# Five input projections a layer from one-pass products of two parts, and a last expert unit by column halves

## The reference, cut to what matters

```
(a_q, a_k, a_v, a_g, a_lr, b_u, c_q, c_k, c_v, c_qi, c_ki, c_wi, d_uv) = split_cols(z, IN_SPLITS)
o_a = gla_mixer(a_q, a_k, a_v, a_g, a_lr, ...)
o_b = pool_mixer(b_u, ...)
o_c = dsa_mixer(c_q, c_k, c_v, c_qi, c_ki, c_wi, rel_bias)   # top 64 keys a query, then attention
o_d = sgu_mixer(d_uv, ...)
h += concatenate([o_a, o_b, o_c, o_d]) @ W_out
```

## Time and profile before

| what | value |
|---|---|
| median of 3 runs | 1337.87 us (1337.4 to 1337.96) |
| the profiled execution | 1337.72 us, of which the span is 1335.9 us |
| PE busy | 1256.2 us (94% of the span) |
| DVE, ACT, POOL busy | 500.4, 379.0, 85.1 us |
| input projections and mixers, layer 0 and layer 1 | about 11 to 137 us, 366 to 486 us |
| dense feed-forward of layer 0 | about 175 to 360 us |
| experts | about 537 us to the end |
| idle time of PE in front of expert matmuls, ended by a DMA | 35.2 and 26.5 us |

### The profile page before, as it was taken

The page is one execution under the profiler, slowest core; times in us unless marked ns, Lnnn a source line. Parts: engine busy times, 40 slices in busy tenths (PEclk is TensorE's granted clock), DMA queues, the critical chain, the costliest instruction groups (busy, mean ns, idle before and its releaser), DMA issues.

```text
span 1335.9 us, 15465 instructions
## 1 busy us (share of the span) xinstructions
PE 1256.2 (94%) x6128; PEld 758.1 (57%) x6128; DVE 500.4 (37%) x886; ACT 379.0 (28%) x603; POOL 85.1 (6%) x69
## 2 busy tenths in 40 slices
PE   8999999999999999999989789889889999999876
PEld 6868888888887787434324224224226888434222
DVE  2736387777653726301001001001006999101002
ACT  2542454444424413101001001001005887101002
POOL 0570000000007300000000000000000000000000
PEclk9999999999999999999999999889889999999999
DMA  9733515442473179799999999999999999899996
GB/s 342 315 126 111 220 54 231 174 163 90 146 294 116 43 276 369 326 428 435 426 434 429 432 429 435 428 432 432 432 432 425 429 427 426 370 428 426 429 429 263
DMA packets 32650, 435.81 MB, mean 326 GB/s; under 512 B 5260, under 2 KB 7376, under 8 KB 9296
## 3 DMA queue, kind: packets, MB, share of 16 engines
q1 hardware_dynamic: 32400, 434.48, 78.4%
q0 software_dynamic: 192, 0.53, 0.1%
HBM read 433.94 MB, written 1.05 MB: 326 GB/s over the span
## 4 chain that ended last, share of the span: by engine, by line
PE 68%; DMA 27%; DVE 2%; ACT 1%; SPq 1%; issue 1%; DVEq 0%
DMA ring<-in_experts 26%; PE bank L2256 14%; PE bank L2349 8%; PE bank L2264 7%; PE bank L1736 7%; PE bank L2133 6%; PE bank L1741 5%; PE bank L1762 4%; PE bank L2137 3%; PE bank L2018 1%; PE bank L2025 1%; PE bank L2019 1%; PE bank L2183 1%; PE bank L2208 1%; DMA ring<-in_packed 1%; ACT r L916 1%
## 5 line engine op out<-in xcount | busy, mean ns | idle before, releaser
L2256 PE MATMUL bank<-ring,xs 128*64 128x512 f32 x1568 | 362.3, 606 | 35.3 <-DMA ring<-in_experts 35.2
L2256 PEld LDWEIGHTS bank<-ring,xs 128*64 128x64 f32 x1568 | 111.0, 139 | 247.9 <-issue 218.2
L1606 DVE TENSOR_TENSOR s_act<-wsT,bank 128x256 f32<-128x256 f32 x49 | 20.6, 421 | 503.4 <-ACT wsT L998 503.4
L2264 PE MATMUL bank<-ring,s_act 128*64 128x512 f32 x736 | 173.7, 612 | 26.6 <-DMA ring<-in_experts 26.5
L2264 PEld LDWEIGHTS bank<-ring,s_act 128*64 128x64 f32 x736 | 53.7, 140 | 132.6 <-issue 120.4
L2133 PE MATMUL bank<-x_both,wf_hi 128*128 128x512 f32 x336 | 118.9, 396 | 0.0
L998 ACT ACTIVATE wsT<-bank 128x256 f32<-128x256 f32 x49 | 18.8, 384 | 331.4 <-PE bank L2208 331.4
L1630 DVE TENSOR_TENSOR w_lo<-ring,w_hi 128x1024 fp32r<-128x1024 f32 x84 | 101.5, 1223 | 12.5 <-ACT w_hi L1056 7.5
L932 ACT ACTIVATE wf_hi<-ring 128x1024 fp32r<-128x1024 f32 x66 | 69.7, 1060 | 96.9 <-PE bank L2133 66.1
L1736 PE MATMUL bank<-xnT,ring 128*128 128x256 f32 (+1 forms) x416 | 94.1, 385 | 2.7 <-DVE xnT L1175 1.1
L1056 ACT ACTIVATE w_hi<-ring 128x1024 fp32r<-128x1024 f32 x84 | 89.0, 1061 | 26.4 <-PE bank L2349 23.6
(11 more groups left out here) (379 smaller groups left out, 1443.9 us busy)
## 6 DMA issues: line engine op xcount, KB each, us to landing
ring<-in_experts SPq DMA_DIRECT2D x93, 2048.0 KB, 20.3
ring<-in_experts SPq DMA_DIRECT2D x36, 4096.0 KB, 25.9
ring<-in_packed SPq DMA_DIRECT2D x18, 1536.0 KB, 6.8
ring<-in_packed SPq DMA_DIRECT2D x11, 2048.0 KB, 13.1
ring<-in_packed SPq DMA_DIRECT2D x18, 1024.0 KB, 5.1
extra<-in_experts SPq DMA_DIRECT2D x3, 2048.0 KB, 9.7
ring<-in_packed SPq DMA_DIRECT2D x2, 656.0 KB, 7.3
ring<-in_packed SPq DMA_DIRECT2D x1, 1312.0 KB, 5.7
```

The costliest lines, as they stand in the source:

```text
L2256: i = mm(ps[d % 2][SMALL * side:SMALL * side + SMALL, :], xs[:, k, :], weights(u)[:, at:at + FC], start=k == 0, stop=k == KT - 1)
L2264: i = mm(ps[6 + half][SMALL * side:SMALL * side + SMALL, :], s_act[:, d % 4, x + side, :], weights(UNIT_OF["out", d, 0])[:, at:at + FC], s ...
```

## The change

1. **Products.** AG, CV, BU, CQ and UV are no longer float32 matmuls. Weights and activations are used as a rounded part (hi) and a rest (lo), and PE makes the products hi·hi, lo·hi and hi·lo in fp32r, in each layer. QI and A stay float32.
2. **New side work.** ACT rounds seven blocks of 128x2048 (ag, cv, bu, cq0, cq1, uv0, uv1) and the two tiles of the activations (x0, x1). In layer 0 POOL subtracts for ag and cv and DVE for bu, cq0, cq1, uv0, uv1, x1, x0; in layer 1 POOL does cq0 and cq1, and DVE the rest. x_lo replaces the float32 activations in place, so it waits until unit A is done.
3. **Order.** PE now runs logit, AG, CV, BU, CQ, attention products, UV t = 1, UV t = 0. DVE's `score_and_take` is cut into `sums`, `take` and `chosen`; the eviction of q comes after the rest parts of uv, the product with `sg` and the rest part of row 2. ACT makes row parts 2 and 3 ahead of 0 and 1; the eviction of uv0 comes after row parts 0 and 1. POOL scales the memory after `wkv` instead of before it, and makes rows 0 and 1 last, in pieces of 512 words.
4. **Slots and loads.** The slots are renamed. The hi part of CQ and of UV lies in the slot of QI and of A; the others' in the free half of their own slot. So `wkv` is loaded when AG is done (before: when QI is done), the output rows 2 and 3 when CV and BU are, rows 0 and 1 when CQ is, `wq` and `wo` when UV is.
5. **End.** The last unit lies in memory by column halves, and the last job loads it in two transfers of 1 MB; half 0 waits for the first alone. The scatter's additions run half by half over both tiles, and the squares are summed for 512 columns at a time: two squares, two small `Identity` steps, then square and root for each tile. A root table is loaded earlier.
6. Some semaphores are merged (`top_diff` with `sel_ready`, `j_yps` with `y_half`).

```diff
-U_A, U_AG, U_CQ, U_CV, U_BU, U_QI, U_UV = SLOTS
-U_WOUT, U_WQ, U_WKV, U_WO = U_A, U_BU, U_QI, U_UV
+U_QI, U_CQ, U_CV, U_BU, U_A, U_AG, U_UV = SLOTS
+U_WOUT, U_WQ, U_WKV, U_WO = SLOTS[0], SLOTS[4], SLOTS[5], SLOTS[6]
+HI_OF = {U_CQ: U_QI, U_UV: U_A}
...
+        HI_ORDER = [("ag", "x1", "x0", "cv", "bu", "cq0", "cq1", "uv0", "uv1", "row2", "row3", "row0", "row1", "row4"),
+                    ("ag", "cv", "bu", "cq0", "cq1", "x1", "x0", "uv0", "uv1", "row2", "row3", "row0", "row1", "row4")]
+        LO_POOL = [("ag", "cv", "wkv", "row0", "row1"), ("cq0", "cq1", "wkv", "row0", "row1")]
+        LO_DVE = [("x1", "x0", "bu", "cq0", "cq1", "uv0", "uv1"), ("ag", "cv", "bu", "x1", "x0", "uv0", "uv1")]
...
SP  -                for i in range(4):
    +                for i in (2, 3, 0, 1):
    +                    if i == 0:
    +                        sp.wait_ge(slot_free[U_CQ], turn[1])
    +                sp.wait_ge(slot_free[U_UV], turn[1])
    +                        if last and u == len(JOB_UNITS) - 1:
    +                            sp.dma_start(into[:, 0:2048], src[:, 0:2048]).then_inc(arrived_half, 16)
    +                            into, src = into[:, 2048:4096], src[:, 2048:4096]
...
ACT +                def hi_of(*parts):
    +                    for part in parts:
    +                        if part[0] == "x":
    +                            t = int(part[1])
    +                            i = act.activation(x_hi[:, t, :, :], x_raw[t], ACT.Copy)
    +                        else:
    +                            act.wait_ge(arrived[IN_PARTS[part][0]], layer * (16 * LAYER_TURNS) + 16)
    +                            i = act.activation(part_hi(part), part_raw(part), ACT.Copy)
    +                        i.then_inc(S["hi_done"], 1)
    +                if layer:
    +                    hi_of("ag", "cv", "bu")
...
DVE +                sums(1, 256)
    +                if layer < 1:
    +                    factors(layer, 2)
    +                take(1, 256)
    +                dve.wait_ge(slot_free[U_A], ended[0])
    +                lo_of("x1", "x0")
    +                sums(0, P)
                     group("logit")
                     dve.tensor_scalar(la, ...).then_inc(S["la_ready"], 1)
    +                take(0, P)
    +                if layer < 1:
    +                    lo_of("bu")
                     ...
    +                chosen(1, 256)
    +                chosen(0, P)
    +                if layer < 1:
    +                    lo_of("cq0", "cq1")
                     ...
    +                out_of("cv", cv[:, :, :], v3(ps[3], 0, 512, 2))
    +                lo_of("uv0", "uv1")
    +                (sg products)
    +                rows_split(2)
                     out_of("q", qT[:, :, :], v3(ps[7], 0, 512, 2))
    +                rows_split(3)
...
PE  +                for t in (1, 0):
    +                    hi_ready(f"x{t}")
    +                    tokens(side(5, t), x_hi[:, t, :, :], wh, t, opens=t == 1)
    +                    lo_ready("ag")
    +                    tokens(side(5, t), x_hi[:, t, :, :], wl, t)
    +                for t in (1, 0):
    +                    lo_ready(f"x{t}")
    +                    i = tokens(side(5, t), x_lo[t], wh, t, closes=True)
    +                i.then_inc(g_ps["ag"], 1)
...
ACT +            for t in range(TT):
    +                act.wait_ge(S["j_cv"], n_jobs * 2 + (t + 1))
    +                link(act.activation(xr[:, t, 0:FC], h[:, t, 0:FC], ACT.Square, accum_out=ss[:, t:t + 1]))
    +            for t in range(TT):
    +                link(act.activation(st[:, 80 + t:81 + t], ss[:, t:t + 1], ACT.Identity, bias=eps[:, :], scale=1.0 / D))
    +            for t in range(TT):
    +                act.wait_ge(S["j_cv"], n_jobs * 2 + (t + 3))
    +                link(act.activation(xr[:, t, FC:D], h[:, t, FC:D], ACT.Square, accum_out=st[:, 82 + t:83 + t]))
    +                act.activation(rms[:, t:t + 1], st[:, 82 + t:83 + t], ACT.Sqrt, bias=st[:, 80 + t:81 + t], scale=1.0 / D)
```

More of the change, by code:

```diff
@@ L715, in _, with lo_of, rows_split @@
                 restart()
+                def lo_of(part):
+                    gp.wait_ge(S["hi_done"], hi_count(layer, part))
+                    gp.tensor_tensor(part_lo(part), part_raw(part), part_hi(part), ALU.subtract).then_inc(S["lo_done"], 1)
+                def rows_split(n):
+                    gp.wait_ge(S["hi_done"], hi_count(layer, f"row{n}"))
+                    for c in range(0, 2048, 512):
+                        i = gp.tensor_tensor(row_lo(n)[:, c:c + 512], ring[:, ROWS[n], c:c + 512], row_hi(n)[:, c:c + 512],
+                                             ALU.subtract)
+                    i.then_inc(S["lo_done"], 1)
+                gp.wait_ge(S["scored"], first)
+                take_wait()
+                if layer < 1:
+                    lo_of("ag")
+                    gp.wait_ge(S["scored"], second)
+                    lo_of("cv")
+                else:
+                    lo_of("cq0")
+                    lo_of("cq1")
                 gp.wait_ge(S["scored"], second)
@@ L852, in _ @@
                 i.then_inc(S["rel"], 1)
+                if layer < 1:
+                    hi_of("cv", "bu")
+                else:
+                    hi_of("uv0", "uv1")
                 out_of("ag", sg[:, :, :], v3(ps[5], 0, 512, 2), ACT.Silu)
+                if layer < 1:
+                    hi_of("cq0", "cq1")
                 act.wait_ge(S["la_ready"], L1)
@@ L1225, in _ @@
                 dve.tensor_tensor_scan(bs, cc("reset"), la, 0.0, mult, add).then_inc(S["b_ready"], 1)
+                chosen(1, 256)
+                chosen(0, P)
+                if layer < 1:
+                    lo_of("cq0", "cq1")
                 dve.wait_ge(S["eb_ready"], L1)
@@ new lines, in _ @@
+                for t in (1, 0):
+                    lo_ready(f"x{t}")
+                    i = tokens(side(5, t), x_lo[t], wh, t, closes=True)
+                i.then_inc(g_ps["ag"], 1)
+                wh, wl = unit_parts(U_CV)
+                hi_ready("cv")
+                pe.wait_ge(S["rel"], second)
+                for t in range(TT):
+                    tokens(side(3, t), x_hi[:, t, :, :], wh, t, opens=t == 0)
+                    tokens(side(3, t), x_lo[t], wh, t)
+                lo_ready("cv")
@@ L1969, in _ @@
                 pe.wait_ge(S["p"], first)
[L1970 removed]
+                pe.wait_ge(g_ev["uv0"], L1)
                 for hh in range(HEADS):
```

336 lines of the change are left out of this document (231 added, 105 removed).

## The result

The changed kernel takes 1343.75 us (median of five executions, 1338.21 to 1345.28), the kernel before 1337.85 us beside it: a ratio of 1.0035, with a 95% interval of 1.0023 to 1.0046. It is slower, by 4.7 us by the ratio and 5.9 by the medians; the forecast was 1325.4 us, 12.5 faster. The execution that was profiled is the fastest of the five, 1338.21 us with a span of 1336.3, 0.4 longer than before. So its trace shows where some 12.9 us went, and not yet why the other four are longer.

The account below looks back on a forecast made before the run. PE bounds the projection stretches of both layers, the weight stream the experts. Layer 0 4.9 + layer 1 7.6 + end 0 = 12.5 us off, giving 1325.4 us from the median; range 1320.5 to 1332.5.

Parts of the forecast that it names:

- Products, what they remove: All five projections: three fp32r products replace one float32 matmul; 0.95 us a group of eight, 8.6 us saved a layer.
- Layer 0 up to UV's end: Layer 0 with its side work: UV ends at 90.6 against 95.5, gaining 4.9 us, bounds 3.9 and 7.6.
- The first gap: Layer 0, before the last CV groups: PE waits 1.5 us for POOL's rest of cv.
- the second: Layer 0, before UV t = 1: PE idles 2.7 us for DVE's eviction of q, taken at 79.5.
- Layer 1 up to UV's end: UV ends at 436.3 against 444.2; layer 1 gains 7.6 us, bounds 5.5 and 8.6.
- The hold of the x parts: Layer 1: DVE's x parts held by POOL's subtraction, x0 ready at 399.5, AG ending at 400.4, not 399.3.
- Behind UV: DVE's chain to the second logits starts later after uv0's eviction, beside kx; 0 us lost, bound 1.
- Rival 3: Whole-instruction holds: subtractions in both layers wait for POOL steps, up to 1.6 us in layer 0; gain 4.9, 1333.0 us; chance 0.17.
- The step of 1.13 us: Layer 0: a short DVE step of 0.29 us took 1.13, ending just after POOL's; counted as held.
- rival 5: POOL starves: kx in layer 0 waits for twelve POOL steps; at 4.6 us each 8 us slower, 1346; chance 0.06.
- Rival 4: The experts absorb the layers' gain, the weight stream not being shifted: no change; chance 0.04.
- The end: Last products, additions, squares and closing steps: sum 0 us, bounds 0.6 gained and 0.4 lost.

Follow-up runs that it names:

- run 1: Changed kernel without POOL's subtractions for rows 0 and 1, PE using their hi part instead of the rest; 1522.32 us, with other experts chosen.
- run 6: Changed kernel with POOL's subtractions of rows 0 and 1 in pieces of 256 columns instead of 512; 1340.87 us, ratio 1.0023 to the kernel before.
- run 7: Changed kernel with POOL's subtraction of rows 0 and 1 as one step of 2048 columns each; 1346.69 us, ratio 1.005 to the kernel before.
- run 8: Kernel before, with only POOL's subtractions of rows 0 and 1 moved to its end, in pieces of 512 columns; 1354.09 us, ratio 1.0112.
- run 3: Changed kernel with unread filler products in PE's waits behind UV (6 and 7 in layer 0, 5 in layer 1); 1339.68 us, ratio 1.0014.
- run 9: The changed kernel measured again, nothing altered; 1341.64 us, ratio 1.0028 to the kernel before.
- run 5: Changed kernel with ACT evicting uv0 before it rounds rows 0 and 1; 1341.25 us, ratio 1.0025 to the kernel before.
- version 2: Changed kernel with DVE, not POOL, subtracting rows 0 and 1 ahead of the moments, ACT rounding them before uv1's eviction; 1328.45 us, ratio 0.9913.
- run 12: version 2 with DVE's eviction of q put ahead of its subtraction of row 2; 1327.5 us, ratio 0.9922 to the kernel before.
- run 10: run 6's kernel with unread filler products in PE's waits behind UV, 11 before the second softmax in each layer; 1337.87 us, ratio 0.9988.
- run 11: run 10's kernel with fillers cut to 6 before the second softmax and none before vn in layer 0; 1334.63 us, ratio 0.9962.

## Why the prediction was wrong, point by point

- **Products, what they remove**: right. Eight fp32r products of 256 columns take 0.94 to 0.96 us (50.07, 51.03, 51.99, 52.93 are the starts of groups), against 0.95 forecast.
- **Layer 0 up to UV's end**: 7.1 us gained where 4.9 was forecast, inside its bounds of 3.9 to 7.6. The first gap, before the last CV groups, was 0.57 us and not 1.5; the second, before UV for DVE's eviction of q, 1.34 and not 2.7. In the other profiles with the same order of DVE the second is 1.2 to 2.4 us. The contention there was over-estimated: DVE's subtractions of row and unit parts took 2.24 to 2.29 us beside POOL's scaling of `wkv`. POOL paid instead (23.14 us for the eight, 12.92 in the earlier trace rows).
- **Layer 1 up to UV's end**: 7.7 us for a forecast of 7.6 (436.3 against 444.2 in its own sum is 7.9). The hold of the x parts was there: 3.95 us for the two at 396.69, and a wait of PE of 0.97 us.
- **Behind UV**, "I keep 0 of loss, bound 1": this is the step that failed. It cost 8.2 and 6.9 us, all of the gain (7.1 and 7.7) in the fastest execution. I had put POOL's rows 0 and 1 there only as work that "ends by 110 at the latest", and asked whether its consumer, the output products, would wait. I never asked what these eight steps do to DVE's list in the same 11 us, though in the same text I took a hold of that kind for the x parts of layer 1 and bounded it for the subtractions before q. Rival 3 had the right mechanism in the wrong place. Before q the subtractions kept their length; DVE's chain of short steps behind UV is where a hold by a whole POOL step triples each. Runs 1, 6, 7 and 8 show it: remove POOL's steps and the layers are short again, change their length and DVE's follows, put them into the old kernel and it loses the same.
- The Trainium skill, page "SBUF — State Buffer", section "SBUF: two separate sides", has a rule that would have given this: a Vector instruction with two SBUF inputs, or in a two-port mode, and a GpSimd one that reads SBUF take a shared port for the whole instruction, and the other waits. Runs 6 and 7 agree for POOL's TENSOR_TENSOR, with DVE at 0.83, 1.37 and 4.63 us; beside POOL's TENSOR_SCALAR they don't, as DVE's lengths above show. The step of 1.13 us that the prediction counts for the rule is a TENSOR_SCALAR with one SBUF tensor as input, so it bears on the two-port clause and not on the one for two inputs. I had set the rule aside for the second and forgotten it for the first.
- **POOL**, rival 5: `kx` was not late in the changed kernel (90.25). Not what happened.
- **Rival 4**, the experts absorb it: no. Over all traces with the same routing the stretch from the first expert product to the end is 798.6 to 802.2 us, whether it starts at 525.20 (798.7) or at 540.03 (798.7). What is gained in the layers comes out at the end. What makes the 3.6 us between executions in that stage is open.
- **The end**: 0.3 us lost in both kernels that have it, within the bounds of 0.6 gained and 0.4 lost. An earlier half could not matter, as the prediction said: the last products still start right behind PE's own work (1321.45 after 1321.09 + 0.44).
- **Clock**: nothing in the forecast. In the kernel before, PE had no idle time behind UV and the clock was at 1.00 there; I did not ask what a gap of 3 us would add to itself. In layer 0 of the fastest execution of the changed kernel that price is about 1 us (6.14 us from the softmax's transposes to the output products, against 5.07 in run 3); runs 9, 5 and 6 show it at 1.8 to 4.1 us in layer 0 alone (6.89, 9.19 and 9.20 us). It may be why the median lies 5.5 us above the profiled execution: the other four executions have a mean granted clock of 0.971 to 0.977, against 0.982. That is not shown. Their traces are not there, and run 3 still spread over 10 us with the clock kept in layer 0.

What the change is worth with this side work on DVE is told by versions 2 and 12: 10 to 12 us faster than the kernel before.

## What to carry to other kernels

When work is moved to another engine's free time, don't ask only who waits for it, but which short steps of the neighbour share a port with it at that time: DVE's chain of 0.4 us steps next to POOL's long two-input steps takes POOL's step length for each. Such work belongs beside a stretch where DVE is idle or reads PSUM, or on DVE itself; if it must stay, short pieces halve the damage to a step (0.83 for 1.37 us), though the time of run 6 was not clearly better for it. And a new wait on PE can cost more than its length: here the granted clock fell to its lower level in or behind such waits, and stayed there for a time that differed from execution to execution. Count it, and take more than one execution before trusting one profile.

## What the runs showed of the hardware that was not expected

- The hold is one for one. The lengths read as if DVE's step starts to move when POOL's running step ends, and gets its turn before POOL's next: 0.77, 1.39 and 4.6 us of POOL gave 0.83, 1.37 and 4.63 us of DVE, and beside only two POOL steps exactly two DVE steps were held in layer 0.
- A DVE TENSOR_SCALAR with one SBUF input of 128x256 is held as well (0.41 to 1.36 us), even one of 128x4 (L1399: 0.17 us before, 0.70 in layer 0 and 1.28 in layer 1). TENSOR_REDUCE (0.69) and steps that read a bank (0.44) are not.
- Beside POOL's TENSOR_SCALAR steps DVE keeps its length within some 0.4 us, and it is POOL that stretches: 12.92 to 23.14 us for eight, and 25.17 in version 2, where DVE subtracts more. POOL's line in the changed kernel:
```profile
58.85 23.14 POOL L792 TENSOR_SCALAR ring<-ring,columns 128x512 f32<-128x512 f32 x8
```
- PE's clock fell to 0.50 in or shortly behind waits of 1.5 us (run 5, layer 1) to 6.6 us (run 7 with 2048 columns), and stayed there for 3 us (run 12) to 20 us (run 7, 106 to 126 us), PE being busy for most of it. A wait of 2.35 us before UV (run 1) left it at 1.00, so the length of a wait alone does not tell. Products nobody reads in the wait kept it at 1.00 (run 3 in layer 0, runs 10 and 11).
